# RWKV-7 triangle inversion on half of the columns, GpSimd clearing the rest, and norms by logarithm and exponential

## The chip, the cores and the metric

The kernel runs on one NeuronCore of a Trainium2 chip. The metric is the device time of one execution in microseconds (us). The median of three executions of the kernel before is 3554.81 us (3553.1 to 3555.05).

## The reference

The model is a trunk of two layers with 256 prompt positions and 8 sequences of 8 new positions, 320 columns in all. Layer 0 mixes with HGRN2 heads and with 16 RWKV-7 heads of 64 channels, layer 1 with retention and RG-LRU; each layer ends in a SwiGLU mixer. Only the RWKV-7 part is touched:

```python
kk = kk / jnp.maximum(jnp.sqrt(jnp.sum(kk * kk, axis=-1, keepdims=True)), 1e-12)
...
sa = jnp.einsum('bhij,bhj->bhi', s, -kk_t)
s = (s * w_t[:, :, None, :] + sa[..., None] * (kk_t * a_t)[:, :, None, :]
     + v_t[..., None] * k_t[:, :, None, :])
...
y = ((y - mean) * lax.rsqrt(var + GN_EPS) * ln_w + ln_b)
```

The kernel computes the recurrence in chunks of 64 positions. In a chunk the vectors `sa` depend on the earlier ones through a strictly triangular 64x64 matrix N, so each chunk and head needs the inverse of a unit triangular matrix. It is built by doubling: at level l (block size 2^l) the inverse of each block of twice that size is made from the two inverses on its diagonal and the part of N between them. In transposed form that adds X_T times N_T times X_T to the upper right quarter of each block, so that of the 64 columns only the second half of each block of 2^(l+1) can receive a value.

## The kernel before

Nearly all of the time is matrix products with streamed weights: weights come in units by DMA, ScalarE rounds a unit to its high part (L295), VectorE and GpSimd subtract to get the low part (L306), and TensorE multiplies (L330, L334, L350, L368).

The RWKV-7 stage lies between two of these, from about 568 to 886 us of the span. No weights are multiplied in it. The 16 heads are worked on in four sets of four heads. Two sets run side by side (x = 0 and 1, each with four of the eight PSUM banks), twice (G = 0 and 1). A pair of sets is called a group below. Each engine has a generator per set (`rwkv_pe`, `rwkv_act`, `rwkv_dve`, `rwkv_pool`) that yields stage numbers; `by_stage` writes the two generators' instructions to the engine's queue in order of stage, set 0 first. So each engine runs a fixed order, and semaphores between engines carry the dependences. `STEPS` names those steps that share one semaphore for each engine; a wait for such a step is a count.

A group runs as follows.
1. Projections and sigmoids (L1520, L1288). DVE forms kk and k, ACT squares kk (L1292), PE sums the squares over each head (L1527). ACT takes the root (L1296). DVE meanwhile makes the bonus product (L1380), a scan (L1383) and a difference (L1385), and then, when both sets are through with these, the maximum with 1e-12 (L1388), the reciprocal (L1389), the product (L1390) and the bonus (L1394). ACT takes three exponentials (L1300 to L1302), GpSimd one product (L1505), DVE four more, up to `til` (L1403).
2. Transposes (L1548) and the chunk matrices (L1560, L1563), masked by DVE into G (L1412) and, as starts of the inversion, into XT, XI and NTm (L1421 to L1426). The tiles nN, XI, XT and T1 lie in the memory of rA, rWB, rE and rKK.
3. The inversion, levels 1 to 5, on blocks of 64x64: ten a set at levels 1 and 2, eight after. A block is two products, one for each half of the partitions (HB). First T1 = N_T X_I (L1591); ACT copies it from PSUM (L1318), while DVE masks the next NTm (L1435); then PE forms the addition to XT (L1599) and, up to level 4, the addition to XI (L1601), and DVE adds both (L1441, L1444). PE does all of a set's blocks in a row, and alternates between the sets: L1591 of set 0, L1591 of set 1, L1599 and L1601 of set 0, then those of set 1.
4. Five chunks (L1629, L1639, L1648 to L1654), the last with 16-column products against the eight states (L1619, stationary 64x64), then states and norms: mean (L1670), square (L1342), variance (L1676), gate (L1680), root by ACT (L1348), reciprocal (L1489) and the rest by DVE (L1490 to L1497), all of set 0 first, then those of set 1. The first step of the next group waits for its end, and after the second group the weights' path waits for it.

Every fp32 product stands in the trace as two weight loads and two matmuls; such a pair of a load and a matmul is called a piece below.

Of the kernel before, what the change touches and what calls it, by code (L numbers as in the profile page):

```python
# [19 lines left out]
T = T_PROMPT + SEQS * T_SEQ  # L20
# [92 lines left out]
def build(nc, d):  # L113

    f32, f32r, i32, u8 = mybir.dt.float32, mybir.dt.float32r, mybir.dt.int32, mybir.dt.uint8
    ALU, ACT, AX = mybir.AluOpType, mybir.ActivationFunctionType, mybir.AxisListType
    mult, add, sub = ALU.mult, ALU.add, ALU.subtract
    ctx = ExitStack()
    with ctx:
# [54 lines left out]
        rms_eps, gn_eps = com[:, 584:585], com[:, 585:586]  # L174
# [9 lines left out]
        o = 2 * T  # L184
# [984 lines left out]
        def f_tile(g, j):  # L1169
# [5 lines left out]
        RJ, RGROUPS, RSTAGES = 2, 4, 74  # L1175
        NBLK = 5 * RJ
# [2 lines left out]


        STEPS = {"act": ("wa", "kk2", "norm", "exp", "n", "sy", "y2", "sd"),
                 "dve": ("kk", "bon", "b", "til", "y4", "yc"),
                 "pe": ("lora", "kkn", "bsum", "n03", "n4", "s0", "mu", "var", "gate")}
        ONCE = {name: (engine, i + 1) for engine, names in STEPS.items() for i, name in enumerate(names)}

# [47 lines left out]
        def blk(r, kind, a, b, n):  # L1233

            return r.nat[a:b, 5 * kind + n // RJ, n % RJ, :]

        def shift_dve(dve):

# [34 lines left out]
        def rwkv_act(act, x):  # L1273
            r = rbuf[x]
            bank = r.bank
            for G in range(RGROUPS // 2):
                g = 2 * G + x
                j0, at0 = RJ * g, G * RSTAGES
                w = lambda name, n: r.wait(act, name, n)
# [7 lines left out]
                for j in range(RJ):  # L1287
                    act.activation(r.WB[:, j, :], bank[j][:, 0:T], ACT.Sigmoid, bias=vec("w0", j0 + j))  # L1288
                    ins = act.activation(r.A[:, j, :], bank[2 + j][:, 0:T], ACT.Sigmoid, bias=vec("a0", j0 + j))
# [1 line left out]
                w("kk", G + 1)  # L1291
                act.activation(r.E[:, :, :], r.KK[:, :, :], ACT.Square).then_inc(r.sem("kk2"), 1)  # L1292
                yield at0 + 4
                w("kkn", G + 1)
                for j in range(RJ):
                    ins = act.activation(r.E[:, j, :], bank[j][:, 0:T], ACT.Sqrt)  # L1296
                ins.then_inc(r.sem("norm"), 1)
                yield at0 + 6
                w("b", G + 1)
                act.activation(r.tAR[:, 1], r.tK[:, :, :], ACT.Exp, scale=WLOG_SCALE)  # L1300
# [12 lines left out]
                for l in range(1, 6):  # L1313
                    yield at0 + 14 + 4 * l
                    w("t1", 5 * G + l)
                    for k in range(2 if l < 3 else 1):
                        n = min(8, NBLK - 8 * k)
                        ins = act.activation(r.T1[:, 8 * k:8 * k + n, :], bank[k][:, 0:64 * n], ACT.Copy)  # L1318
                    ins.then_inc(r.sem("t1s"), 1)
                for c in range(5):  # L1320
                    a = at0 + 37 + 5 * c
                    if c == 4:
# [22 lines left out]
                yield at0 + 71  # L1345
                w("var", G + 1)
                for j in range(RJ):
                    ins = act.activation(r.YSQ[:, j, :], bank[j][:, 0:T], ACT.Sqrt, bias=gn_eps)  # L1348
                ins.then_inc(r.sem("sd"), 1)

        def transposed(copy, r, q, *how):

# [7 lines left out]
        def rwkv_dve(dve, x):  # L1360
            r = rbuf[x]
            bank = r.bank
            L = lambda ins: link(dve, "dve", ins)
            for G in range(RGROUPS // 2):
# [14 lines left out]
                for j in range(RJ):  # L1379
                    ins = dve.scalar_tensor_tensor(r.BV[:, j, :], rr[:, j, :], vec("r_k", j0 + j), k[:, j, :], mult, mult)  # L1380
                ins.then_inc(r.sem("bon"), 1)
                for j in range(RJ):
                    ins = dve.tensor_tensor_scan(r.tK[:, j, :], rscan, r.WB[:, j, :], 0.0, mult, add)  # L1383
                L(ins)
                dve.tensor_tensor(r.WB[:, :, :], r.tK[:, :, :], r.WB[:, :, :], sub)  # L1385
                yield at0 + 5
                w("norm", G + 1)
                L(dve.tensor_scalar(r.E[:, :, :], r.E[:, :, :], 1e-12, None, ALU.max))  # L1388
                L(dve.reciprocal(r.E[:, :, :], r.E[:, :, :]))  # L1389
                dve.tensor_tensor(r.KK[:, :, :], r.KK[:, :, :], r.E[:, :, :], mult).then_inc(r.sem("b"), 1)  # L1390
                yield at0 + 6
                w("bsum", G + 1)
# [6 lines left out]
                dve.scalar_tensor_tensor(r.tAR[:, 0], r.KK[:, :, :], -1.0, r.tAR[:, 0], mult, mult)  # L1399
                dve.tensor_tensor(r.tAR[:, 1], rr, r.tAR[:, 1], mult)  # L1400
                dve.tensor_tensor(r.tK[:, :, :], k, r.E[:, :, :], mult)
                w("kka", G + 1)
                dve.tensor_tensor(r.tB[:, :, :], r.tB[:, :, :], r.E[:, :, :], mult).then_inc(r.sem("til"), 1)  # L1403
                for q in range(1, 8, 2):
                    yield at0 + (9 if q < 4 else 11)
# [23 lines left out]
                for l in range(1, 6):  # L1429
                    nb = NBLK if l < 3 else 4 * RJ  # L1430
                    if l < 5:
                        yield at0 + 14 + 4 * l
                        w("t1", 5 * G + l)
                        nx = NBLK if l + 1 < 3 else 4 * RJ
                        dve.tensor_tensor(cj(r.NTm, nx), nt[:, 0:nx // RJ], mask(m_up[l + 1], nx), mult)\  # L1435
                           .then_inc(r.sem("ntm"), 1)
                    yield at0 + 16 + 4 * l
                    w("xu", 5 * G + l)
                    for k8 in range((nb + 7) // 8):
                        n = min(8, nb - 8 * k8)  # L1440
                        ins = dve.tensor_tensor(r.XT[:, 8 * k8:8 * k8 + n], r.XT[:, 8 * k8:8 * k8 + n],  # L1441
                                                bank[2 + k8][:, 0:64 * n].rearrange("p (n t) -> p n t", t=64), add)
                        if l < 5:
                            ins = dve.tensor_tensor(r.XI[:, 8 * k8:8 * k8 + n], r.XI[:, 8 * k8:8 * k8 + n],  # L1444
                                                    bank[k8][:, 0:64 * n].rearrange("p (n t) -> p n t", t=64), add)
                    ins.then_inc(r.sem("x"), 1)
                    w("x", 5 * G + l)

# [37 lines left out]
                ins.then_inc(r.sem("yc"), 1)  # L1486
                yield at0 + 72
                w("sd", G + 1)
                L(dve.reciprocal(r.YSQ[:, :, :], r.YSQ[:, :, :]))  # L1489
                L(dve.tensor_tensor(r.Y[:, :, :], r.Y[:, :, :], r.YSQ[:, :, :], mult))  # L1490
                for j in range(RJ):
                    ins = dve.tensor_scalar(r.Y[:, j, :], r.Y[:, j, :], vec("ln_w", j0 + j), vec("ln_b", j0 + j), mult, add)
# [7 lines left out]
        def rwkv_pool(pool, x):  # L1500
            r = rbuf[x]
            for G in range(RGROUPS // 2):
                yield G * RSTAGES + 6
                r.wait(pool, "b", G + 1)
                pool.tensor_tensor(r.tB[:, :, :], r.KK[:, :, :], r.A[:, :, :], mult).then_inc(r.sem("kka"), 1)  # L1505

        def rwkv_pe(pe, x):
            r = rbuf[x]
# [2 lines left out]
            for G in range(RGROUPS // 2):  # L1511
# [68 lines left out]
                for l in range(1, 6):  # L1580
                    nb = NBLK if l < 3 else 4 * RJ
                    yield at0 + 13 + 4 * l
                    w("ntm", 5 * G + l)
                    if l == 1:
                        w("gm", 5 * (G + 1))
                        w("n", G + 1)
                    else:
                        w("x", 5 * G + l - 1)
                    for n in range(nb):
                        for a, b in HB:  # L1590
                            ins = mm(bank[n // 8][a:b, 64 * (n % 8):64 * (n % 8) + 64], r.NTm[a:b, n], r.XI[a:b, n],  # L1591
                                     start=True, stop=True)
                    ins.then_inc(r.sem("t1"), 1)
                    yield at0 + 15 + 4 * l
                    w("t1s", 5 * G + l)
                    for n in range(nb):
                        for a, b in HB:
                            o = slice(64 * (n % 8), 64 * (n % 8) + 64)
                            ins = mm(bank[2 + n // 8][a:b, o], r.T1[a:b, n], r.XT[a:b, n], start=True, stop=True)  # L1599
                            if l < 5:  # L1600
                                ins = mm(bank[n // 8][a:b, o], r.XT[a:b, n], r.T1[a:b, n], start=True, stop=True)  # L1601
                    ins.then_inc(r.sem("xu"), 1)
                for c in range(5):
                    cs = slice(64 * c, 64 * c + 64)
# [772 lines left out]
```

## Time and profile before

| | |
|---|---|
| median of three executions | 3554.81 us |
| the profiled execution | 3554.26 us |
| its span | 3552.4 us |
| PE busy | 3317.8 us (93%) |
| DVE busy | 1914.1 us (54%) |
| ACT busy | 1223.8 us (34%) |
| POOL busy | 1509.9 us (43%) |
| granted TensorE clock, mean | 0.961 of full |
| DMA | 474.99 MB, mean 134 GB/s |

The profiled execution takes 1.9 us more than its span; this lies before the first and after the last recorded instruction. A busy share is over the whole span and hides the stages. The page's line of the DMA rate falls from about 140 GB/s to between 8 and 45 GB/s in the slices from 533 to 888 us: this is the RWKV-7 stage, with no weights streamed. The line PEclk is the clock that was granted to TensorE, in tenths of full speed; it is lowest there, too.

### The profile page before, as it was taken

The numbers are of one execution on the slowest core, as the hardware profiler recorded it, in microseconds if no ns is written. First come the engines' busy times: TensorE is split into PE (matmuls) and PEld (weight loads), VectorE is DVE, ScalarE is ACT, GpSimd is POOL, SyncE is SP. The second block draws the span as 40 slices with busy tenths as digits, with TensorE's granted clock in tenths as the row PEclk, the third lists the DMA queues.
The fourth block names the chain that finished last, engine by engine and source line by source line (L and its number), as shares of the span: only waits on it lengthen the run. The fifth ranks groups of instructions, "written<-read, shape, count | busy, mean of one in ns | idle before, by whom it ended". The sixth has DMA issues, their size and how long they took to land.

```text
span 3552.4 us, 63012 instructions
## 1 busy us (share of the span) xinstructions
PE 3317.8 (93%) x24576; PEld 3200.6 (90%) x24576; DVE 1914.1 (54%) x2439; ACT 1223.8 (34%) x1512; POOL 1509.9 (43%) x854
## 2 busy tenths in 40 slices
PE   7999996857989999999999899998989999999997
PEld 7999995746979999999999899986989999999997
DVE  6553556485775442254446687736774432344466
ACT  4444453132343332233322434432343332333322
POOL 3555771000434444444443246732334445444443
PEclk9999997978989999999999899999999999999998
DMA  4444341000434444444444364444434444444443
GB/s 170 137 138 139 118 144 45 8 21 18 163 107 143 152 148 155 141 149 148 148 156 152 97 210 131 162 169 175 148 101 153 146 158 147 141 148 148 157 148 110
DMA packets 118671, 474.99 MB, mean 134 GB/s; under 512 B 13424, under 2 KB 15088, under 8 KB 115568
## 3 DMA queue, kind: packets, MB, share of 16 engines
q1 hardware_dynamic: 108864, 421.58, 37.2%
q10 hardware_dynamic: 9648, 51.17, 3.7%
q8 instruction: 115, 1.88, 0.2%
q14 instruction: 44, 0.36, 0.0%
HBM read 450.66 MB, written 22.03 MB: 133 GB/s over the span
## 4 chain that ended last, share of the span: by engine, by line
PE 86%; DVE 8%; ACT 3%; issue 2%; POOL 1%; ACTq 0%; DMA 0%; DVEq 0%; POOLq 0%
PE ps L330 49%; PE ps L334 25%; PE ps L350 1%; ACT w_hi L295 1%; PE ps L1119 1%; PE ps L2076 1%; PE ps L1599 1%; POOL w_lo L306 1%; PE ps L368 1%; DVE w_lo L306 1%; PE ps L1563 1%; PE ps L1601 0%; PE ps L1548 0%; PE ps L1773 0%; DVE rE L1389 0%
## 5 line engine op out<-in xcount | busy, mean ns | idle before, releaser
L306 POOL TENSOR_TENSOR w_lo<-raw,w_hi 128x512 fp32r<-128x512 f32 (+2 forms) x756 | 1441.7, 1908 | 1821.0 <-ACT w_hi L295 1812.1
L330 PE MATMUL ps<-x_hi,w_hi 128*128 128x320 f32 x4832 | 1444.4, 313 | 11.9 <-ACT w_hi L295 4.0
L330 PE MATMUL ps<-x_lo,w_hi 128*128 128x320 f32 x4832 | 1433.8, 310 | 0.0
L295 ACT ACTIVATE w_hi<-raw 128x1024 fp32r<-128x1024 f32 (+1 forms) x756 | 840.0, 1112 | 1587.2 <-PE ps L334 1515.5
L330 PEld LDWEIGHTS ps<-x_hi,w_hi 128*128 128x128 f32 x4832 | 914.1, 189 | 22.6 <-ACT w_hi L295 10.7
L330 PEld LDWEIGHTS ps<-x_lo,w_hi 128*128 128x128 f32 x4832 | 913.5, 189 | 0.9
L306 DVE TENSOR_TENSOR w_lo<-raw,w_hi 128x512 fp32r<-128x512 f32 (+1 forms) x592 | 554.1, 937 | 634.6 <-ACT w_hi L295 623.9
L334 PE MATMUL ps<-x_hi,w_lo 128*128 128x320 f32 x4832 | 816.1, 311 | 23.5 <-DVE w_lo L306 16.1
L334 PEld LDWEIGHTS ps<-x_hi,w_lo 128*128 128x128 f32 x4832 | 739.8, 189 | 28.1 <-issue 15.6
L330 PE MATMUL ps<-u_hi,w_hi 128*128 128x320 f32 x1408 | 415.5, 309 | 8.3 <-DVE u_lo L762 8.3
L330 PE MATMUL ps<-u_lo,w_hi 128*128 128x320 f32 x1408 | 415.0, 309 | 0.0
L330 PEld LDWEIGHTS ps<-u_hi,w_hi 128*128 128x128 f32 x1408 | 264.3, 188 | 9.3 <-DVE u_lo L762 9.3
L330 PEld LDWEIGHTS ps<-u_lo,w_hi 128*128 128x128 f32 x1408 | 264.3, 188 | 0.0
L334 PE MATMUL ps<-u_hi,w_lo 128*128 128x320 f32 x1408 | 227.3, 309 | 0.0
L334 PEld LDWEIGHTS ps<-u_hi,w_lo 128*128 128x128 f32 x1408 | 211.7, 188 | 0.0
L728 ACT ACTIVATE gate<-gate 128x320 f32<-128x320 f32 x88 | 41.5, 472 | 262.9 <-DVE gate L748 262.9
L753 DVE TENSOR_TENSOR stat<-ps,srow 128x320 f32<-128x320 f32 x88 | 43.2, 491 | 151.0 <-PE ps L334 151.0
L748 DVE TENSOR_TENSOR gate<-ps,srow 128x320 f32<-128x320 f32 x88 | 43.2, 491 | 133.2 <-PE ps L334 133.0
L350 PE MATMUL ps<-x_hi,w_hi 128*128 128x320 f32 x192 | 51.9, 394 | 59.9 <-ACT x_hi L719 25.4
L760 DVE CAST u_hi<-stat 128x320 f32 (+1 forms) x88 | 101.3, 1152 | 12.0 <-DVE stat L756 11.4
L350 PEld LDWEIGHTS ps<-x_hi,w_hi 128*128 128x128 f32 x192 | 40.0, 249 | 67.5 <-issue 52.2
L400 DVE COPY M<-ps 128x320 f32<-128x320 f32 (+1 forms) x64 | 31.4, 491 | 127.0 <-PE ps L334 118.4
(412 smaller groups left out, 2807.7 us busy)
## 6 DMA issues: line engine op xcount, KB each, us to landing
raw<-in_w_ffn_in SPq DMA_DIRECT2D x352, 512.0 KB, 3.5
raw<-in_w_ffn_out SPq DMA_DIRECT2D x128, 704.0 KB, 4.1
raw<-in_w_in_even SPq DMA_DIRECT2D x116, 512.0 KB, 3.5
raw<-in_w_in_odd SPq DMA_DIRECT2D x96, 512.0 KB, 3.5
raw<-in_w_out_even SPq DMA_DIRECT2D x32, 512.0 KB, 3.5
raw<-in_w_out_odd SPq DMA_DIRECT2D x32, 512.0 KB, 3.5
hS<-in_state_hgrn ACTq DMA_DIRECT2D x4, 1024.0 KB, 5.0
out_hgrn_s<-hS ACTq DMA_DIRECT2D x4, 1024.0 KB, 3.8
```

The lines of the kernel that those rows point to most:

```text
L295: nc.scalar.activation(w_hi[s % 2][:, 0:g.kt, :], raw[s % 4][:, 0:g.kt, :], ACT.Copy)\
L306: eng.tensor_tensor(w_lo[s % 2][:, k0:k1, :], raw[s % 4][:, k0:k1, :], w_hi[s % 2][:, k0:k1, :].bitcast(f32), sub).then_inc(sem(f"split_lo ...
L330: nc.tensor.matmul(out, w_hi[s % 2][:, k, :], x[:, kk, :], start=half == 0 and k == 0 and x is xh, stop=False)
L334: mm = nc.tensor.matmul(out, w_lo[s % 2][:, k, :], xh[:, half * g.kt + k, :], start=False, stop=half == 1 and k == g.kt - 1)
L350: nc.tensor.matmul(outs[t], w_hi[s % 2][:, k + a, :], x[:, kk + a, :], start=kk + a == 0 and x is xh, stop=False)
L368: mm = nc.tensor.matmul(outs[t], w_lo[s % 2][:, k, :], xh[:, half * g.kt + k, :], start=False, stop=half == 1 and k == g.kt - 1)
L728: act.activation(gate[:, p % 2, :], gate[:, p % 2, :], ACT.Silu).then_inc(sem("gate"), 1)
L748: dve.tensor_tensor(gate[:, p % 2, :], PS[(g.tile0 + 2 * p) % 4][:, 0:T], srow, mult)\
L753: dve.tensor_tensor(uf, PS[(g.tile0 + 2 * p + 1) % 4][:, 0:T], srow, mult).then_inc(sem("tile_out"), 2)
L760: dve.tensor_copy(hi, uf).then_inc(sem("u_dve"), 1)
L1119: ins = mm(PS[b0][:, o:o + P], x[:, j, cs], x[:, j, cs], start=True, stop=True)
L1563: ins = mm(o[a:b, 128 * j:128 * j + 128].rearrange("p (a t) -> p a t", a=2), (r.tB, r.tK)[i][a:b, j, cs], r.tAR[a:b, :, j, cs], start=True ...
```

## The change

The inversion computes only the columns that can be nonzero. L1591 takes as its moving operand the first half of the columns of each block of XI, 32 instead of 64. Its result is packed into one bank (ten blocks x 32 columns are 320), and ACT spreads it into those columns of T1. L1599 takes the second half of the columns of XT, L1601 the first half of the columns of T1. The stationary operand stays 64x64 in each, so T1's other half has to be zero: GpSimd clears it before level 1 (320 elements a partition, after `til`), and for each later level the quarter of T1 that is newly outside (160 elements), after the products of the level before. PE waits for this ahead of L1599. DVE adds half as many elements, in one instruction each instead of two at levels 1 and 2.

The norms: 1/max(sqrt(s), 1e-12) becomes exp(-0.5 ln(max(s, 1e-24))). DVE takes the maximum out of PSUM, in two instructions a set, ahead of the scan, with a new semaphore step `kks`. ACT takes Ln and Exp of 640 elements each. 1/sqrt(var + eps) becomes Ln (two instructions a set) and Exp. The maximum and the two reciprocals of the old path on DVE (L1388, L1389, L1489) go.

```diff
-                 "dve": ("kk", "bon", "b", "til", "y4", "yc"),
+                 "dve": ("kk", "bon", "kks", "b", "til", "y4", "yc"),
...
+        def half_columns(t, nb, l, h):
+            return t[:, 0:nb, :].rearrange("p n (q h s) -> p (n q) h s", h=2, s=1 << l)[:, :, h, :]
+        def half_moving(t, a, b, n, l, h):
+            return t[a:b, n, :].rearrange("p (q h s) -> p q h s", h=2, s=1 << l)[:, :, h, :]
+        def half_bank(bank, n, l):
+            return bank[:, 0:32 * n].rearrange("p (m s) -> p m s", s=1 << l)
...  rwkv_act
-                w("kkn", G + 1)
-                for j in range(RJ):
-                    ins = act.activation(r.E[:, j, :], bank[j][:, 0:T], ACT.Sqrt)
-                ins.then_inc(r.sem("norm"), 1)
+                w("kks", G + 1)
+                act.activation(r.E[:, :, :], r.E[:, :, :], ACT.Ln).then_inc(r.sem("ln"), 1)
+                w("ln", 2 * G + 1)
+                act.activation(r.E[:, :, :], r.E[:, :, :], ACT.Exp, scale=-0.5).then_inc(r.sem("norm"), 1)
...
-                    for k in range(2 if l < 3 else 1):
-                        n = min(8, NBLK - 8 * k)
-                        ins = act.activation(r.T1[:, 8 * k:8 * k + n, :], bank[k][:, 0:64 * n], ACT.Copy)
-                    ins.then_inc(r.sem("t1s"), 1)
+                    nb = NBLK if l < 3 else 4 * RJ
+                    if l == 1:
+                        w("til", G + 1)
+                    act.activation(half_columns(r.T1, nb, l, 0), half_bank(bank[0], nb, l), ACT.Copy)\
+                       .then_inc(r.sem("t1s"), 1)
...
-                    ins = act.activation(r.YSQ[:, j, :], bank[j][:, 0:T], ACT.Sqrt, bias=gn_eps)
-                ins.then_inc(r.sem("sd"), 1)
+                    ins = act.activation(r.YSQ[:, j, :], bank[j][:, 0:T], ACT.Ln, bias=gn_eps)
+                ins.then_inc(r.sem("ln"), 1)
+                w("ln", 2 * G + 2)
+                act.activation(r.YSQ[:, :, :], r.YSQ[:, :, :], ACT.Exp, scale=-0.5).then_inc(r.sem("sd"), 1)
...  rwkv_dve, ahead of the scan
+                w("kkn", G + 1)
+                for j in range(RJ):
+                    ins = dve.tensor_scalar(r.E[:, j, :], bank[j][:, 0:T], 1e-24, None, ALU.max)
+                ins.then_inc(r.sem("kks"), 1)
...
-                L(dve.tensor_scalar(r.E[:, :, :], r.E[:, :, :], 1e-12, None, ALU.max))
-                L(dve.reciprocal(r.E[:, :, :], r.E[:, :, :]))
...
-                w("kka", G + 1)
+                w("kka", 6 * G + 1)
...
+                    xt, xi = half_columns(r.XT, nb, l, 1), half_columns(r.XI, nb, l, 0)
+                    ins = dve.tensor_tensor(xt, xt, half_bank(bank[2], nb, l), add)
+                    if l < 5:
+                        ins = dve.tensor_tensor(xi, xi, half_bank(bank[0], nb, l), add)
...
-                L(dve.reciprocal(r.YSQ[:, :, :], r.YSQ[:, :, :]))
...  rwkv_pool
+                for l in range(1, 6):
+                    yield G * RSTAGES + (12 if l == 1 else 14 + 4 * l - 2)
+                    if l == 1:
+                        r.wait(pool, "til", G + 1)
+                        z = half_columns(r.T1, NBLK, 1, 1)
+                    else:
+                        r.wait(pool, "xu", 5 * G + l - 1)
+                        z = r.T1[:, :, :].rearrange("p n (q i h s) -> p (n q) i h s", i=2, h=2, s=1 << (l - 1))[:, :, 1, 0, :]
+                    pool.memset(z, 0.0).then_inc(r.sem("kka"), 1)
...  rwkv_pe
-                            ins = mm(bank[n // 8][a:b, 64 * (n % 8):64 * (n % 8) + 64], r.NTm[a:b, n], r.XI[a:b, n],
-                                     start=True, stop=True)
+                            o = bank[0][a:b, 32 * n:32 * n + 32].rearrange("p (q s) -> p q s", s=1 << l)
+                            ins = mm(o, r.NTm[a:b, n], half_moving(r.XI, a, b, n, l, 0), start=True, stop=True)
...
+                    w("kka", 6 * G + 1 + l)
...
-                            ins = mm(bank[2 + n // 8][a:b, o], r.T1[a:b, n], r.XT[a:b, n], start=True, stop=True)
+                            ins = mm(o, r.T1[a:b, n], half_moving(r.XT, a, b, n, l, 1), start=True, stop=True)
                             if l < 5:
-                                ins = mm(bank[n // 8][a:b, o], r.XT[a:b, n], r.T1[a:b, n], start=True, stop=True)
+                                ins = mm(p, r.XT[a:b, n], half_moving(r.T1, a, b, n, l, 0), start=True, stop=True)
```

## Rows read from the trace of the kernel before

**Rows 1.** The chain of waits from 560 to 910 us, its shares by line.

```profile
by line: issue 6.9%; PE ps L1599 6.2%; PE ps L1563 5.1%; PE ps L1601 5.1%; PE ps L1548 5.0%; DVE rE L1389 4.8%; PE ps L1591 4.1%; PE ps L1619 4.1%; PE ps L350 3.2%; PE ps L1648 2.5%; DVE ySQ L1489 2.5%; PE ps L1649 2.5%; DVE XT L1441 2.3%; 
```

**Rows 2.** DVE's timeline, norm of the first group: start us, duration us, engine, line, operation.

```profile
584.47 1.53 DVE L1383 TENSOR_TENSOR_SCAN tK<-evc,rWB 128x320 f32<-128x320 f32 x2
...
586.78 0.48 DVE L1388 TENSOR_SCALAR rE<-rE 128x640 f32<-128x640 f32 x1
...
597.68 1.67 DVE L1394 TENSOR_TENSOR BV<-ps,Z 128x320 f32<-128x320 f32 x4
```

**Rows 3.** ACT's timeline in the HGRN2 stage: a logarithm, and the exponential after it.

```profile
476.15 1.28 ACT L904 ACT_TABLE_LOAD   x1
477.44 0.74 ACT L904 ACTIVATE Z<-Z 128x640 f32<-128x640 f32 x1
...
481.62 1.28 ACT L918 ACT_TABLE_LOAD   x1
```

**Rows 4.** Chain of waits, last norm, first group: start us, duration us, what.

```profile
711.62 1.28 ACT L1348
...
713.89 4.16 DVE ySQ L1489
...
725.62 0.84 DVE rY L1490
```

**Rows 5.** Chain of waits: first and last piece of the inversion, both groups.

```profile
631.12 2.40 PE ps L1591 x40
...
665.67 0.70 DVE XT L1441
...
787.32 2.40 PE ps L1591 x40
...
820.69 0.70 DVE XT L1441
```

**Rows 6.** Groups of instructions, 560 to 910 us: form and count, busy us, mean ns, idle.

```profile
L1599 PE MATMUL ps<-XT,T 64*64 64x64 f32 x704 | 40.4, 224 | 0.0
...
L1601 PE MATMUL ps<-T,XT 64*64 64x64 f32 x576 | 36.1, 224 | 0.0
...
L1591 PE MATMUL ps<-XI,NTm 64*64 64x64 f32 x704 | 28.6, 239 | 19.2 <-DVE XI L1426 13.3 <-DVE XI L1444 6.0
```

**Rows 7.** Chain of waits from 631 to 640 us: four pieces, at either clock.

```profile
634.42 0.21 PE ps L1599 x4
...
638.34 0.12 PE ps L1599 x4
```

**Rows 8.** Timeline of weight loads ahead of narrow products, merged, last one's latency included.

```profile
688.37 0.54 PEld L1619 LDWEIGHTS ps<-tAR,rS 64*64 64x64 f32 x8
...
692.41 1.08 PEld L1619 LDWEIGHTS ps<-tAR,rS 64*64 64x64 f32 x9
...
175.31 1.31 PEld L1141 LDWEIGHTS ps<-hQ,hS 128*128 128x128 f32 x11
```

**Rows 9.** Windows: length, busy of PE, PEld, DVE, ACT, POOL, clock, DMA share, GB/s.

```profile
631.00:636.00 5.00, 4.88 (x91) 4.89 (x93) 1.71 (x3) 0.77 (x2) 0.00 (x0) 0.50 0.02 3
636.00:640.00 4.00, 4.00 (x132) 4.00 (x130) 1.83 (x5) 0.00 (x0) 0.00 (x0) 0.91 0.00 0
...
690.00:693.00 3.00, 3.00 (x52) 3.00 (x52) 0.00 (x0) 0.33 (x1) 0.00 (x0) 0.72 0.00 0
...
845.00:848.00 3.00, 3.00 (x39) 3.00 (x37) 0.00 (x0) 0.36 (x1) 0.00 (x0) 0.50 0.00 0
```

**Rows 10.** PE's timeline at level 3, second set, with the idle time before it.

```profile
649.67 1.15 PE L1591 MATMUL ps<-XI,NTm 64*64 64x64 f32 x32 [1.00 <-DVE XI L1444]
```

**Rows 11.** POOL's groups of instructions: the smallest long operation.

```profile
L1252 POOL TENSOR_TENSOR Z<-Z,shd 128x255 f32<-128x255 f32 x26 | 20.9, 802 | 0.0
```

**Rows 12.** Chain of waits: the same step of two chunks after the inversion.

```profile
671.71 0.45 PE ps L1639 x8
...
677.43 0.45 PE ps L1639 x8
```

More of the change, by code:

```diff
@@ L1438, in rwkv_dve @@
                     w("xu", 5 * G + l)
[L1439 to L1445, printed above, removed]
+                    xt, xi = half_columns(r.XT, nb, l, 1), half_columns(r.XI, nb, l, 0)
+                    ins = dve.tensor_tensor(xt, xt, half_bank(bank[2], nb, l), add)
+                    if l < 5:
+                        ins = dve.tensor_tensor(xi, xi, half_bank(bank[0], nb, l), add)
                     ins.then_inc(r.sem("x"), 1)
@@ L1595, in rwkv_pe @@
                     w("t1s", 5 * G + l)
+                    w("kka", 6 * G + 1 + l)
                     for n in range(nb):
                         for a, b in HB:
-                            o = slice(64 * (n % 8), 64 * (n % 8) + 64)
-                            ins = mm(bank[2 + n // 8][a:b, o], r.T1[a:b, n], r.XT[a:b, n], start=True, stop=True)
+                            o, p = (bank[k][a:b, 32 * n:32 * n + 32].rearrange("p (q s) -> p q s", s=1 << l)
+                                    for k in (2, 0))
+                            ins = mm(o, r.T1[a:b, n], half_moving(r.XT, a, b, n, l, 1), start=True, stop=True)
                             if l < 5:
-                                ins = mm(bank[n // 8][a:b, o], r.XT[a:b, n], r.T1[a:b, n], start=True, stop=True)
+                                ins = mm(p, r.XT[a:b, n], half_moving(r.T1, a, b, n, l, 0), start=True, stop=True)
                     ins.then_inc(r.sem("xu"), 1)
```

## The prediction, written before the changed kernel ran

> **What bounds the kernel now.** I read the chain of waits of the RWKV-7 stage first. No engine owns it: DVE's two reciprocal lines hold 7.3% of it, the three lines of the inversion (L1591, L1599, L1601) 15.4% [rows 1]. So the stage is a relay, and each edit has to be weighed at its place in it. Second, the timelines and the chain around the two norms show reciprocals one after the other, with the rest waiting [rows 2, 4]. Third, the chain of the inversion gives its first and last piece: 34.55 us in the first group, 33.37 us in the second, nearly all of it TensorE [rows 5]. Last, I asked at what clock that engine works there, and what a piece (one weight load and one matmul) costs at either clock [rows 7 to 9].
>
> **First norm.** Between L1388 of set 0 and L1394 DVE spends 597.68 - 586.78 = 10.90 us: twice a maximum of 0.48, twice a reciprocal of 4.16, and two products for the rest, 1.62 [rows 2, 4]. The reciprocals and the old maxima go. Four maxima out of PSUM come, ahead of the scans; the nearest row is L1394, four PSUM reads of 320 columns in 1.67 us. The new sum is 1.67 + 1.62 = 3.3, so 7.6 us go. ACT must keep up: after set 1's maximum, DVE still has that set's scan and difference (586.78 - 584.47 = 2.31) and set 0's product (0.81), 3.1 in all. ACT needs Ln 0.74, a table load 1.28 and Exp 0.74, 2.76 together [rows 2, 3]. That just fits, and the margin of 0.3 is why I take 7.5 a group, 15.0 in all (bounds 11 and 16: the lower has each group 2 us late). DVE's new wait for the head sums (`kkn`) has the scan, and then all of the next set's products, behind it. They are done in time in the first group, and I charge nothing for it.
>
> **Last norm.** Now: ACT's table load at 711.62, the roots, the first reciprocal at 713.89, and the second set's first product at 725.62 [rows 4]. After: load 1.28, two logarithms 0.99 (711.62 + 1.28 to 713.89, as the roots now), load 1.28, Exp 0.74; set 0 goes on at 715.9. For set 1 the same four, 4.3 us, so its product starts at 720.2. The 3.4 us of DVE's work on set 0 fit into that. So 725.6 - 720.2 = 5.4 us go, 10.9 in two groups (bounds 9 and 15). All of it is on the path: the next group and the next weights wait for set 1's end.
>
> I count a table load at each change between Ln and Exp because the HGRN2 stage has one at its Ln and one more at the Exp after it, 1.28 us each [rows 3]. The Trainium skill ("ScalarE: Activation LUTs", section "Table sets: the hidden batching unit") says that Ln followed by Exp needs one load, since one set has both. By that rule the last norm is bound by DVE, ends 2 us sooner a group, and the sum is 4 to 5 us lower. The trace speaks for the second load.
>
> **The inversion's products.** The count of pieces stays: 704 + 576 + 704 = 1984, 992 a group [rows 6]. Each moves 32 columns instead of 64. Four pieces take 0.12 us at the full clock (2.4 GHz) and 0.21 at the half (1.2 GHz) [rows 7]. Two of the four are on each half of the partitions, at the same time, so a half takes one piece in 58 ns, or in 107. L1619 has the same stationary operand but 16 columns: with one half at work, seven steps between its weight loads take 0.54 less the last one's 0.14, 58 ns each; at the half clock eight steps take 1.08 - 0.22, 107 ns each. L1141, with 128 stationary columns and 8 moving, takes 112 ns [rows 8]. A piece costs what its weight load costs, and 64 moving columns just hide behind it. So 32 buy nothing. Bounds for a piece: 0 and 14% less, the latter if both halves' loads were to interleave better at 25 ns a piece; I take 0, as the rows with 16 columns do.
>
> **The clock.** Here I expect the loss. The inversion starts at the half clock in both groups, since PE stands idle while DVE forms XT and XI (13.3 us over both groups for L1426, [rows 6]). At 631 to 636 it has the half, and only after dense 64-column products does it get the full clock, 0.91 in the next stretch [rows 9]. The only long stretch in this stage with narrow moving operands is L1619. There PE and PEld are busy 3.00 of 3.00 us, and the clock falls: 0.72 at 690 to 693, and 0.50 at 845 to 848 [rows 9]. The new inversion stands between the two: 32 columns on each half for each weight load, half of the streaming of now, and double L1619's or more. It would have to rise from the half clock, which these rows show only after dense 64-column products. I take it that it stays at 1.2 GHz up to the chunks.
>
> The Trainium skill ("TensorE: Matmul & The Clock Gate", section "Part 1: The HAM clock gate (the "warmup" mystery)") says that the gate watches how busy PE has been, and that a busy one gets full rate. Taken as busy time, this speaks against me: the new inversion has PE busy all through, the clock would rise as now, and the time would be that of the first rival. L1619 is this trace's evidence that a busy share of 1 isn't enough.
>
> At 53 ns a piece, from the first piece of set 1 on (952 of them, no idle time, since DVE's, ACT's and POOL's shares fit behind 1.7 to 4.2 us of the other set's products): 50.5 us, against 34.55 and 33.37 [rows 5]. That is 16.0 + 17.1 = 33.1 us more. The last addition of XT is 256 elements instead of 512, some 0.3 less a group. Sum of the inversion: +32.5 (bounds -6.6 and +34).
>
> **The chunks after it** start at the half clock, too. A chunk takes 677.43 - 671.71 = 5.72 us for 128 pieces, 3.7 us at the full clock [rows 12]. At the half clock they are 6.8, and with some 0.8 of waits 7.6. These are dense 64-column products, of the kind after which the clock rises. I take that it does in the first or second chunk: +1.3 a group, +2.6 (bounds 0 and +14, the latter if all chunks run at the half clock).
>
> **GpSimd's clearing.** No row has a memset of this size there. POOL's two-input operation of 255 elements takes 0.80 us [rows 11]; for 160 or 320 elements I take 1.0 at most, and 0.1 at least. Set 0's must come between its products of one level and those of the next, behind 4.2 us of set 1's products and both sets' L1591. It hides, and so costs 0; it costs if the clearing were above 7 us (4.5 at the full clock). What would wait behind it in PE's queue is L1599, and all else of both sets. POOL's other work, L1505 and the split for the next weights, is ahead of it or later. The table and state DMAs on ACT's queue aren't moved past anything.
>
> **DVE's and ACT's halves.** Now PE idles 6.0 us for L1444 over both groups [rows 6], a gap of 1.00 before L1591 of set 1 [rows 10]. With half of the elements DVE is through before set 0's L1591 ends. At the half clock this is already in the count of no idle time; at the full clock it is the gain of 6.0.
>
> **The sum.** -15.0 - 10.9 + 32.5 + 2.6 = +9.2 us on the profiled execution's 3554.26, so 3563.5. That execution is 0.55 below the median, so I predict 3564 for the median.
>
> **Rivals.**
> - *The clock rises in the inversion as it does now* (the other side). For it: 32 columns on both halves stream twice or more what L1619 does, and PE never pauses. Against it: L1619 at full busy share lost the clock, and even the 64 columns of now have the half clock up to 636 us, after a start with pauses [rows 9]. The time: -15.0 - 10.9 - 6.0 - 0.6 = -32.5, that is 3522. It decides from the point where the clock rises: each 1 us that the inversion runs at the full clock gives back 0.8, and the change breaks even at 12 of the 101 us.
> - *The clock rises late or only in one group*, or pieces are cheaper than the weight load: 3530 to 3555.
> - *The chunks keep the half clock as well*: their products have pauses, and 64 columns with pauses is what held the half clock at the start of the inversion. 3564 + 11 = 3575.
> - *The change doesn't do what it says on TensorE but the clock is as now*, with DVE or POOL late: the norms' 25.9 alone, 3529. It needs a clearing above 4.5 us, for which nothing speaks.
>
> **How the numbers follow.** Half clock through the inversion 0.64, its own range 3556 to 3571 from the bounds of the norms; chunks slow too 0.08; late rise 0.14; as now 0.12; norms alone 0.02. A measurement of this kernel can tell about 0.2% (7 us) from no change: slower means above 3562, faster below 3548. Of the first case 0.70 is slower, 0.26 the same. With the second case whole and a little of the third, slower 0.54, same 0.21, faster 0.25. The range reaches from 3530, into the late rise and short of the rival of the full clock, to 3576.
>
> **What the profile of the changed kernel will show.** The granted clock in the inversion: 0.50 in the windows after its first products proves the loss, 1.00 there proves me wrong and the first rival right. Four pieces of L1599's successor at 0.12 at the full clock and 0.21 at the half prove the weight load; less would prove columns count. L1394's successor 7.5 us sooner after the scan, with ACT's Ln ahead, proves the first norm, and table loads before each Ln and each Exp prove the count. No idle time of PE put down to POOL proves the clearing free. What would make the prediction wrong most of all is the clock.

## The result, and the profile after

The changed kernel takes 3571.32 us, median of 5 runs (3566.25 to 3571.98), against 3553.1 (3552.53 to 3555.05) for the kernel before on the same chip: a ratio of 1.0047, 95% interval 1.0033 to 1.0062. It is slower, by some 18 us. The profiled execution is the fastest of the five, 3566.25, with a span of 3564.4 against 3552.4: 12.0 us more.

The clock in the inversion comes first. Windows of the changed kernel (columns as in [rows 9]), group 0 and then group 1:

```profile
623.00:640.00 17.00, 16.99 (x319) 16.99 (x320) 4.80 (x8) 1.34 (x3) 0.49 (x2) 0.50 0.01 3
640.00:660.00 20.00, 20.00 (x380) 20.00 (x379) 5.36 (x11) 1.15 (x3) 0.92 (x4) 0.50 0.01 2
660.00:679.00 19.00, 18.90 (x340) 18.58 (x338) 3.27 (x8) 2.53 (x8) 0.46 (x2) 0.50 0.01 3
679.00:697.00 18.00, 16.98 (x415) 16.17 (x412) 3.25 (x12) 4.86 (x18) 0.00 (x0) 0.99 0.01 3
...
804.00:824.00 20.00, 20.00 (x381) 20.00 (x379) 5.36 (x11) 1.15 (x3) 0.92 (x4) 0.50 0.01 2
...
843.00:861.00 18.00, 16.98 (x416) 16.17 (x414) 3.31 (x12) 4.89 (x19) 0.00 (x0) 0.99 0.01 4
```

In the middle of the inversion TensorE is busy 20.00 of 20.00 us and granted 0.50, 1.2 GHz, and it has the half clock from the first product until some 5 us into the first dense chunk (0.50 up to 679.00). Before, it rose some 10 us into group 0's inversion [rows 9]. The groups of PE, 560 to 910 us, answer to [rows 6]:

```profile
L1623 PE MATMUL ps<-XT,T 64*64 64x32 f32 x704 | 68.4, 291 | 0.0
L1625 PE MATMUL ps<-T,XT 64*64 64x32 f32 x576 | 61.1, 291 | 0.0
L1614 PE MATMUL ps<-XI,NTm 64*64 64x32 f32 x704 | 40.1, 291 | 13.1 <-DVE XI L1443 13.1
```

The counts are those of before, each product moves half of the columns, and its mean rose from 224 (L1591: 239) to 291 ns. The 6.0 us of idle time for L1444 are gone, the 13 us ahead of the inversion are not. Its ends, from PE's and DVE's timelines (duration in the second column), answer to [rows 5]:

```profile
623.01 2.35 PE L1614 MATMUL ps<-XI,NTm 64*64 64x32 f32 x40 [1.83 <-DVE XI L1443]
...
674.12 0.42 DVE L1457 TENSOR_TENSOR XT<-XT,ps 128x256 f32<-128x256 f32 x1 [1.28 <-PE ps L1623]
...
787.07 2.13 PE L1614 MATMUL ps<-XI,NTm 64*64 64x32 f32 x36 [1.82 <-DVE XI L1443]
...
838.18 0.42 DVE L1457 TENSOR_TENSOR XT<-XT,ps 128x256 f32<-128x256 f32 x1 [1.29 <-PE ps L1623]
```

That is 51.1 us in each group, where it was 34.55 and 33.37. The last norm of group 0 on ACT, and the products that wait for it on DVE, answer to [rows 4]:

```profile
723.14 1.28 ACT L1361 ACT_TABLE_LOAD   x1
724.44 0.94 ACT L1361 ACTIVATE ySQ<-ps,com 128x320 f32<-128x320 f32 x2
725.40 1.28 ACT L1364 ACT_TABLE_LOAD   x1
726.69 0.74 ACT L1364 ACTIVATE ySQ<-ySQ 128x640 f32<-128x640 f32 x1
727.45 1.28 ACT L1361 ACT_TABLE_LOAD   x1
...
729.71 1.28 ACT L1364 ACT_TABLE_LOAD   x1
```

```profile
727.46 0.82 DVE L1503 TENSOR_TENSOR rY<-rY,ySQ 128x640 f32<-128x640 f32 x1 [5.11 <-ACT ySQ L1364]
...
731.77 0.82 DVE L1503 TENSOR_TENSOR rY<-rY,ySQ 128x640 f32<-128x640 f32 x1 [0.86 <-ACT ySQ L1364]
```

From the first load to set 1's product it is now 8.63 us, before 725.62 - 711.62 = 14.00. DVE around the first norm of group 0 answers to [rows 2]:

```profile
583.52 0.88 DVE L1399 TENSOR_SCALAR rE<-ps 128x320 f32<-128x320 f32 x2
584.32 1.53 DVE L1402 TENSOR_TENSOR_SCAN tK<-evc,rWB 128x320 f32<-128x320 f32 x2
...
586.63 1.55 DVE L1407 TENSOR_TENSOR rKK<-rKK,rE 128x640 f32<-128x640 f32 x2
588.10 1.68 DVE L1411 TENSOR_TENSOR BV<-ps,Z 128x320 f32<-128x320 f32 x4
```

Scan to L1411 is 3.78 us, before 13.21; less the four maxima out of PSUM that now stand ahead of the scans (1.6), 7.8 are gone. Some of it is lost again right behind. The first copy after L1411 (L1397 before, L1414 now), from DVE's timelines before and after, and GpSimd's products from POOL's timeline after:

```profile
599.28 0.16 DVE L1397 COPY PC<-tAR 128x8 f32<-128x8 f32 x1
```

```profile
589.69 1.42 DVE L1414 COPY PC<-tAR 128x8 f32<-128x8 f32 x1
```

```profile
587.59 3.49 POOL L1518 TENSOR_TENSOR tB<-rKK,rA 128x640 f32<-128x640 f32 x2 [34.57 <-DVE rKK L1407]
```

And in group 1, where DVE now waits for the head sums:

```profile
741.97 0.89 DVE L1399 TENSOR_SCALAR rE<-ps 128x320 f32<-128x320 f32 x2 [0.65 <-PE ps L1549]
```

The 12.0 us by stage, from the starts of the first product of the inversion, the first product of the chunks (L1629, now L1653) and the last norm's first table load:

| stretch | before | after | change |
|---|---|---|---|
| up to the first inversion | 626.94 | 618.84 | -8.1 |
| inversion, group 0 | 38.54 | 54.96 | +16.4 |
| chunks, group 0 | 46.14 | 49.34 | +3.2 |
| last norm, first norm of group 1 | 71.52 | 59.76 | -11.8 |
| inversion, group 1 | 37.36 | 54.97 | +17.6 |
| chunks, group 1 | 47.67 | 49.22 | +1.6 |
| last norm and all that follows | 2684.23 | 2677.31 | -6.9 |

The first row holds 1.8 us that aren't the change's: DVE's first product of the stage that reads ACT's sigmoid (L1376, now L1391) starts at 577.15 before and 575.37 after, and up to there the two kernels run the same instructions. From that product to the inversion it is 49.79 us before and 43.47 after, -6.3; in group 1 (from 732.57 and 738.73) 50.57 and 44.17, -6.4. The start of the stage differs by chance: DVE's L1371 and its successors start at 568.12 before, and in the traces of the changed kernel and of the eleven below at 566.1 to 566.4 in six and at 568.9 to 569.1 in the six others.

### The profile page after: what moved, and what is told of

It is laid out like the page before. It is cut to its first block, busy times and chain, and to the rows that moved or that the text cites. A ratio compares the mean times of both kernels' runs of the same rounds, so it can differ in the third digit from the quotient of the medians.

```text
span 3564.4 us, 63043 instructions
## 1 busy us (share of the span) xinstructions
PE 3358.6 (94%) x24576; PEld 3241.4 (91%) x24576; DVE 1873.4 (53%) x2419; ACT 1238.9 (35%) x1519; POOL 1516.9 (43%) x874
## 4 chain that ended last, share of the span: by engine, by line
PE 69%; DVE 4%; issue 1%; ACT 1%; DMA 0%; ACTq 0%; DVEq 0%
PE ps L330 43%; PE ps L334 22%; PE ps L350 1%; PE ps L2100 1%; PE ps L368 1%; PE ps L1797 0%; DVE M L666 0%; DVE w_lo L306 0%; ACT w_hi L295 0%; DVE X L634 0%; DVE X L635 0%; DVE x_lo L645 0%; DVE x_lo L488 0%; PE ps L2086 0%; DVE X L704 0%
## 5 line engine op out<-in xcount | busy, mean ns | idle before, releaser
L330 PEld LDWEIGHTS ps<-x_hi,w_hi 128*128 128x128 f32 x4832 | 912.2, 189 | 23.4 <-ACT w_hi L295 11.5
L334 PE MATMUL ps<-x_hi,w_lo 128*128 128x320 f32 x4832 | 812.9, 311 | 23.5 <-DVE w_lo L306 16.1
L429 DVE TENSOR_SCALAR M<-M,vecs 128x320 f32<-128x320 f32 x64 | 97.1, 1517 | 2.2
```

The costliest lines, as they stand in the source:

```text
L330: nc.tensor.matmul(out, w_hi[s % 2][:, k, :], x[:, kk, :], start=half == 0 and k == 0 and x is xh, stop=False)
L334: mm = nc.tensor.matmul(out, w_lo[s % 2][:, k, :], xh[:, half * g.kt + k, :], start=False, stop=half == 1 and k == g.kt - 1)
L429: dve.tensor_scalar(m, m, vec(w[0], KT * w[1] + t), None, mult).then_inc(sem("tile_w"), 1)
```

## Experiments

All are compared with the kernel before on the same chip. "Inversion" with two times is the stretch called so in the table, of the profiled execution, in groups 0 and 1; before it was 38.5 and 37.4.

### The two parts, each alone

**norms**: the kernel before, with the lines on Ln, Exp, `kks`, the maxima and the reciprocals changed as in the diff, and nothing else.

> The kernel before with the part on norms alone (log and exp in place of square root and reciprocal, both norms); the inversion as before. Theory (the half clock in the inversion is the whole loss): this is the kernel before less the two norms' terms of the prediction, -15.0 and -10.9, 3553.1 - 25.9 = 3527. Rival (norms are swallowed, since what comes after is later or since the clock rises later in the inversion): 3540 or more.

3532.05 us (3526.7 to 3537.2), ratio 0.9934 [0.9920, 0.9947], inversion 38.5 and 37.6 us: 23 us faster, 3 short of the 26 expected, and within the spread of its own runs.

**inversion**: the changed kernel with the norms put back.

```
-  act.activation(r.E, r.E, ACT.Ln); w("ln", ...); act.activation(r.E, r.E, ACT.Exp, scale=-0.5)
+  act.activation(r.E[:, j, :], bank[j][:, 0:T], ACT.Sqrt)      # DVE: max, reciprocal
```

> The kernel before with the part on the inversion alone (half of the columns on TensorE, ScalarE and VectorE, GpSimd clears); norms by square root and reciprocal as before. If the parts add up, this is 3571.3 + 25.9 = 3597, 44 above the kernel before, and the granted clock is half from before the first product of the inversion to the first chunk in both groups. By the prediction's own terms (+35) it would be 3588. Rival (the norms brought the half clock, the stages standing otherwise than before): the clock rises in the inversion here, and the time is 3553 or less.

3592.9 us, ratio 1.0108 [1.0093, 1.0124], inversion 55.0 and 55.0 us. The parts give -23 and +38, together +15, where the whole change gives +18: they add up within their intervals (some 5 us each way). The norms didn't bring the half clock.

### What in the inversion costs

**stream64**: the changed kernel, TensorE's operands as before.

```
-  ins = mm(o, r.NTm[a:b, n], half_moving(r.XI, a, b, n, l, 0), ...)     # and both updates
+  ins = mm(o64, r.NTm[a:b, n], r.XI[a:b, n], ...)
```

> The changed kernel, but TensorE moves all 64 columns of each piece as in the kernel before; ScalarE copies half, GpSimd clears the rest and VectorE adds half, as in the changed kernel. Theory (fewer columns moved keep TensorE at the half clock, nothing else of the change costs): the clock rises some 10 us into the inversion of group 0 and earlier in group 1, as in the kernel before, x1 to the last add of XT takes 33 to 34.5 us, and the time is 3553.1 - 25.9 - 4 to 7 for the shorter copies and adds, about 3522. Rival (the clearing, its waits or the strided copies and adds are what costs): stays at 3560 or more.

**wide**: besides, ACT copies all, and GpSimd clears nothing.

> Norms by log and exp; TensorE and ScalarE work on all 64 columns as in the kernel before and GpSimd clears nothing; only VectorE adds just the half of the columns that can change. Theory: 3553.1 - 25.9 - about 3 for the shorter adds, 3524, within 3 us of the run with all columns moved and half copied; it beats both kernels. Rival (the clearing and its waits cost something of their own): over 3 us below that run.

3528.2 us (ratio 0.9926 [0.9912, 0.9939]) and 3525.9 (0.9918 [0.9905, 0.9932]). Twice as many columns through TensorE, and 43 us less. The first is 6 us above the 3522 expected, the second 2 above its 3524; the norms alone were 5 above their 3527. Windows of group 0 of the former:

```profile
622.00:631.00 9.00, 6.61 (x129) 6.42 (x131) 6.25 (x8) 1.02 (x4) 0.00 (x0) 0.54 0.01 2
631.00:655.00 24.00, 23.41 (x779) 22.98 (x775) 11.23 (x30) 2.70 (x9) 1.89 (x8) 1.00 0.02 4
```

The clock rises as before. The two differ by less than their runs spread, so the clearing costs nothing that shows. Inversions of 35.1 and 35.1, and 36.0 and 34.8 us, against 38.5 and 37.6 with the norms alone, say what VectorE's halves are worth (with ACT's, in stream64): some 3 us a group.

**contig32**: the 32 columns side by side. These are other columns than the inversion needs, so this kernel computes wrong numbers there; it is of use for its time alone.

```
-  half_moving(r.XI, a, b, n, l, 0)
+  r.XI[a:b, n, 0:32]                       # and so for XT, T1 and the bank
```

> The changed kernel, but each piece moves 32 columns that stand side by side and writes them side by side, instead of every second run of 2^l columns; so it computes other numbers in the inversion. Theory (the number of columns a piece decides): within 5 us of the changed kernel, 3571, half clock up to the chunks. Rival (the strided operand or the strided write is slow or keeps the clock down): the clock rises in the inversion, 3550 or less.

3569.9 us, ratio 1.0045 [1.0031, 1.0060], inversion 55.0 and 55.0: the strides cost nothing. What is left between this kernel and stream64 is the number of columns that a product moves.

### When do 32 columns keep the clock, and when don't they?

**early** and **late**: 32 columns at levels 1 and 2 alone, and at levels 3 to 5 alone (`if l < 3` around the two forms of operand).

> The changed kernel with half of the columns at levels 1 and 2, and all 64 at levels 3 to 5: the converse. Theory (the clock stands at half as long as only 32 columns a piece come, and dense products raise it wherever they stand): the clock rises some 10 us after the start of level 3, not before; 480 pieces at 53 ns, then 190 more at it, then 320 at 29 ns, 45 us a group where the run with all columns had 35.9 and 34.8: 3525.9 + 19 = 3545. Rival (once a pause has put it down, it stays down up to the chunks): 3570.

> The changed kernel with all 64 columns at levels 1 and 2, and half at levels 3 to 5, which the clock reaches at its full level. What a 32-column piece costs at the full clock is read here. If it is the weight load's time, 29 ns, as with 64 columns, and the clock is held: 3526 to 3528. If the clock falls there: levels 3 to 5 are 512 pieces a group, 25 ns more each, 12.8 us, and the chunks 1.4, so 3528 + 28 = 3556. If 32 columns were cheaper at the full clock and held it: below 3523.

early 3544.25 us, ratio 0.9969 [0.9957, 0.9981]; late 3523.2, ratio 0.9913 [0.9898, 0.9927]. Windows, first early (levels 1 and 2, then level 3 on), then late (levels 1 and 2 from the pause on, then 3 to 5):

```profile
621.00:648.00 27.00, 24.75 (x460) 24.62 (x462) 10.09 (x16) 1.79 (x4) 0.72 (x3) 0.50 0.01 2
648.00:651.00 3.00, 3.00 (x61) 3.00 (x60) 0.89 (x2) 0.00 (x0) 0.23 (x1) 0.50 0.03 8
651.00:665.00 14.00, 13.85 (x460) 13.64 (x458) 5.78 (x12) 2.30 (x6) 0.92 (x4) 0.99 0.02 4
```

```profile
619.00:626.00 7.00, 4.88 (x89) 4.69 (x91) 5.18 (x8) 0.69 (x3) 0.00 (x0) 0.53 0.00 0
626.00:637.00 11.00, 10.90 (x367) 10.79 (x364) 5.06 (x15) 1.32 (x6) 0.72 (x3) 0.99 0.02 5
637.00:652.00 15.00, 14.50 (x485) 14.25 (x482) 6.79 (x16) 1.92 (x5) 1.16 (x5) 1.00 0.02 4
```

The work of levels 3 to 5 shows both sides: dense, it raises the clock that 27 us of narrow work had left down; narrow, it keeps a clock that dense work had raised. In early the clock rose 2 us after level 3 began (649.08) in group 0 and some 3 in group 1, not the 10 expected. And 485 narrow products in 14.50 us of work are 30 ns each, dense ones 367 in 10.90 (30 ns): at the full clock 32 columns cost what 64 cost.

**mixed**: 64 columns in the first product of each level, 32 in the updates.

> The changed kernel with all 64 columns in the first product of each level (NTm with XI) and half in the two updates. Open question: does a stretch of some 4 us with 64 columns between stretches of 8 us with 32 raise the clock? If it is the mean over the inversion that counts, two thirds of the way from half to all, it rises in the first 20 us: 3530 to 3545. If each short stretch is judged by itself and none is long enough, it stays at half: 3571. If 4 us are enough: 3528 as with all columns.

3531.7 us, ratio 0.9937 [0.9922, 0.9952], the first of the three answers by its time; that a mean is what counts isn't shown by it. The clock rose some 19 us after the first product in group 0 (inversion 39.7 us) and within 10 in group 1 (34.7). Group 0:

```profile
622.00:640.00 18.00, 16.23 (x305) 16.04 (x303) 7.66 (x12) 1.52 (x6) 0.49 (x2) 0.50 0.01 2
641.00:661.00 20.00, 19.73 (x660) 19.40 (x658) 8.58 (x18) 2.75 (x8) 1.39 (x6) 1.00 0.02 5
```

**filled_narrow**: products that nobody reads, in the pause ahead of the inversion.

```
+  for k in range(2 if x else 4):
+      mm(bank[3][:, :], bones, r.G[:, 0].rearrange("p i j a t -> p (i j a t)"), start=True, stop=True)
   w("ntm", 5 * G + l)                      # level 1, after the waits for gm and n
```

> The changed kernel, with idle time of TensorE before the inversion filled by products whose result nobody reads (64 rows or more by 512 columns, four ahead of set 0's first product and two ahead of set 1's), so that the inversion's 32-column products begin at the full clock. Open question: can 32 columns a piece hold the clock that they could not raise? Theory A (they can't hold it either): the granted clock is 0.50 again after the first products and the time is 3560 or more, within 5 us of the changed kernel less the stretch that was warm. Theory B (they only can't raise it): 1.00 up to the chunks; a group's 992 pieces at 29 ns take 28.8 us instead of 51.1 and the chunks are 1.4 us shorter, so 3571.3 - 2 x 23.7 = 3524.

Neither theory, but both: six runs gave 3540.5, 3540.55, 3540.06, 3521.06, 3524.54 and 3516.7 (ratio of all 0.9929 [0.9908, 0.9950]). The profiled execution, one of the slower three, shows each outcome once (group 0 entered, group 0 on, group 1):

```profile
619.00:626.00 7.00, 5.92 (x135) 4.58 (x136) 5.80 (x8) 0.93 (x2) 0.00 (x0) 1.00 0.01 2
627.00:671.00 44.00, 44.00 (x831) 44.00 (x829) 11.12 (x23) 3.18 (x8) 1.88 (x8) 0.50 0.01 3
...
781.00:813.00 32.00, 30.75 (x965) 29.10 (x966) 16.24 (x29) 4.11 (x10) 1.89 (x8) 1.00 0.02 4
```

Nearly the same instructions with the same pauses (1.10 and 1.09 us ahead of set 0's first product) took 52.6 us in one group and 33.0 in the other. The 19.6 us between them are as much as lies between the mean of the slower three and that of the faster three, and the mean granted clock over the span is 0.961 in each of the slower and 0.966 to 0.969 in the faster. That the faster ones kept the clock in both groups is likely by this, but no trace shows one of them. So after 1 us pauses 32 columns kept the clock once and lost it once; what tips them isn't shown. The Trainium skill ("TensorE: Matmul & The Clock Gate", section "Part 1: The HAM clock gate (the "warmup" mystery)") says that the gate's windows run free of the kernel, so that one kernel can be granted the clock at different points from run to run. This agrees, but no run here steers the phase.

**filled_wide** and **filled_late**: the same filling ahead of wide and of late.

> The run with all 64 columns on TensorE and ScalarE and half on VectorE (3525.9), with the same filling of TensorE's idle time ahead of the inversion. The filler occupies only the 4.7 us and 1.8 us in which TensorE stands idle (four products of 0.85 us, two of 0.85 us). If the clock then is full from the first product, the 7 to 10 us at the half clock at the start of the inversion are gone, some 4 us a group: 3518. Rival (the pause that is left, or the filler's own time, eats it): 3526 or more.

> All 64 columns at levels 1 and 2 and half at levels 3 to 5 (3523.2 without filling), with the idle time of TensorE ahead of the inversion filled as in the earlier runs. With all columns the filling took 2.5 and 1.3 us off the inversions of the two groups; here the inversions took 34.65 and 34.85 us and should take 33.2 each: 3523.2 - 3.1 = 3520. Rival (32 columns are at the edge of what holds the clock, as in the filled run with 32 columns throughout, where group 0 lost it and group 1 kept it): some executions lose it at levels 3 to 5, 3532 or more, and the spread of the runs is 10 us or more.

3523.7 us (ratio 0.9913 [0.9900, 0.9926]) and 3525.7 (0.9913 [0.9900, 0.9927]), each some 6 us above the 3518 and 3520 expected. The inversions fell to 33.5 and 33.5, and to 33.4 and 33.7 us, at the full clock throughout, as expected of filled_late; filled_wide's 8 us were my guess of 4 a group where 2.5 and 1.3 lay. The whole times don't show even this gain: wide, late and both filled ones lie from 3523.2 to 3525.9, within what their runs spread (up to 8 us). The best kernels are these, 0.8 to 0.9% faster than the one before; among them I can't rank. filled_late didn't lose the clock in the execution shown, but its rival's 3532 was neither reached nor its spread of 8 us small enough to exclude a part of it.

## Why the prediction was right

The forecast of 3564 with "slower" at 0.54 came true, as the half clock through the inversion. The measured 3571.3 is 7 us above it, at the upper end of the 3556 to 3571 that the prediction gave this case. By its steps:

- **The clock, the step that decides: right.** Half clock to the first chunk in both groups; with all 64 columns moved (stream64) the clock rises, with 32 (the changed kernel, inversion, contig32) it doesn't. The evidence used, L1619 with 16 columns [rows 9], pointed right, but to less than it seemed to: 32 columns raised the clock in no group that was seen, yet kept it in most that entered at full. The forecast needed the first alone, since both groups begin at half.
- **A piece costs its weight load: right.** 53 ns at half (380 in 20.00 us, above) and 30 at full (late), whether 32 or 64 columns are moved. The section on the clock gate of the Trainium skill that the prediction cites, taken as busy time, would have had the clock rise at a busy share of 1.00; the windows above say no. What it says of a busy engine holds here for dense products only.
- **The inversion: +32.5 predicted, +34.0 measured.** Set 1's first piece to the last addition took 51.1 us, 50.5 predicted.
- **First norm, -7.5 a group: mis-sized by 1.2 and 1.1.** The reciprocals' time is gone as forecast and ACT keeps up, -7.8 in group 0 from DVE's rows. But up to the inversion it is -6.3 in group 0 and -6.4 in group 1. The -8.1 of the table's first row comes near the forecast by luck, as 1.8 of it lie ahead of the stage. Two things went uncounted. The first set's copy on DVE, L1414, took 1.42 us instead of 0.16 in both groups. It ends at 591.11 and 755.18, GpSimd's products L1518 at 591.08 and 755.15; before, GpSimd was as good as through when the copy came. That DVE stood behind GpSimd is likely, no run tests it. And in group 1 the wait for the head sums (`kkn`), which the prediction put at nothing after a look at group 0 alone, cost 0.65 us.
- **Last norm, -5.4:** 14.00 to 8.63 in group 0, 14.00 to 8.62 in group 1, -5.4 each. The other 1.5 of the last stretch's -6.9 lie after the norm, outside the stage. The norms' sum is thus -23.5 in this trace, where -25.9 was predicted and the run with the norms alone gave -23.
- **A table load at each change, four a norm and group: right**, 1283 ns each. The rule of the Trainium skill that the prediction cites, one load for both, was not what this kernel got.
- **Chunks, +2.6 predicted, +4.8 measured: mis-sized by 2.2.** From the first chunk's first product to L1619's (now L1643's) first it took 22.8 and 22.7 us, before 21.1 and 21.2, so the chunks themselves gave +3.2. The rest is group 0's, where the stretch of L1619's successor ran longer at the half clock; before and after:

```profile
686.00:700.00 14.00, 14.00 (x240) 12.66 (x237) 3.60 (x9) 2.15 (x7) 0.00 (x0) 0.76 0.04 12
```

```profile
696.00:712.00 16.00, 16.00 (x242) 14.19 (x238) 3.80 (x10) 2.15 (x7) 0.00 (x0) 0.68 0.04 10
```

Some 240 products take 14 us at 0.76 and 16 at 0.68, in group 1 16 both times. The prediction had looked at the chunks' own products alone.

- **GpSimd's clearing: nothing, right, and smaller than its bounds.** Nothing of PE's waits is put down to it:

```profile
L1527 POOL MEMSET T<- 128x160 f32 x16 | 3.8, 235 | 134.7 <-PE ps L1625 134.7
L1527 POOL MEMSET T<- 128x320 f32 x4 | 1.5, 387 | 12.8 <-DVE tB L1420 12.8
```

- **What the sum missed:** it gave +9.2, the profiled execution +12.0: inversion +1.5, chunks +2.2 and norms +2.4 more than forecast, and 3.3 us less outside the stage (1.8 ahead of it, 1.5 after it), which no term holds. That the sum lies within 3 us is in part luck. The medians give +18. The profiled execution is 5 us below the median of its kind. contig32's has every landmark of the inversions within 0.2 us of the changed kernel's, and its span is 3.9 longer, all after the stage. Most of it falls behind one pause: after the same 2.73 us without work the clock is lost in contig32 and not in the changed kernel, and the products that follow fall a further 2.7 us behind. PE's timeline and a window, first of contig32, then of the changed kernel:

```profile
1062.95 2.47 PE L334 MATMUL ps<-x_hi,w_lo 128*128 128x320 f32 x8 [2.73 <-DVE w_lo L306]
...
1060.00:1070.00 10.00, 7.27 (x32) 7.08 (x31) 4.06 (x5) 1.06 (x1) 2.78 (x2) 0.66 0.37 114
```

```profile
1062.59 1.41 PE L334 MATMUL ps<-x_hi,w_lo 128*128 128x320 f32 x8 [2.73 <-DVE w_lo L306]
...
1060.00:1070.00 10.00, 7.41 (x49) 7.29 (x50) 5.07 (x7) 2.44 (x3) 2.44 (x2) 1.00 0.47 155
```

So a few us hang on whether such a stretch is met. The other four runs of the changed kernel have a mean clock of 0.950 to 0.951 where the profiled one has 0.952; that such stretches explain them is likely by this, not shown.

## What to carry to other kernels

Halving what a product moves gains nothing where its weight load sets the pace, and on TensorE it can cost a factor of two, as here, where an engine busy 20.00 of 20.00 us stayed at 1.2 GHz: ask of each stretch at what clock it is entered, and whether its densest part comes early. Cut the columns on the other engines, whose time does fall (VectorE's halves, 3 us a group), and on TensorE only behind a dense stretch, if at all. Two changes of opposite sign in one diff should be timed apart: the norms alone were worth 23 us. And look for each wait in every group before it is put at nothing.

## What the runs showed of the hardware that was not expected

- Raising the clock and keeping it are different things. 32 columns a piece on each half of the rows never raised it, in 51 us of the changed kernel, inversion and contig32 and 27 us of early, two groups each; entered at full, they kept it in both groups of late and of filled_late and lost it once in two groups of filled_narrow.
- One kernel had two times some 19 us apart on one core (filled_narrow), and in its trace one stretch of the same work took 52.6 or 33.0 us with the clock.
- A VectorE copy of 8 elements a partition took 1.42 us instead of 0.16 in both groups and ended within 0.03 us of the end of a GpSimd two-input operation.
- A GpSimd memset of 320 elements a partition takes 0.39 us and one of 160 0.24, half or less of the 0.80 of the two-input operation of 255 [rows 11].
